# One more attention job of logits ahead of the values: three jobs behind instead of two

## The chip, the cores and the metric

The program runs on one core of a Trainium2 chip. The time is the device time of one execution in microseconds (us), from start to end on that core. Engines are named as in the profile: PE (TensorE) multiplies matrices, DVE (VectorE) and POOL (GpSimd) do elementwise work, ACT (ScalarE) evaluates functions, SP (SyncE) issues transfers. Each engine works through its own instructions in order and waits on semaphores where the program says so.

## The reference

One layer of a hybrid encoder over 2048 prompt tokens and 32 sample tokens that continue a stream of 1024. What matters here is the attention branch: for each query, an indexer scores all visible keys, the best 256 are kept, and eight heads (two key heads with four query heads each) attend to those keys with a relative-position bias.

```python
score = jnp.einsum('bqh,bqhk->bqk', wiblk, jax.nn.relu(dots)) * INDEX_SCALE
_, sel = lax.top_k(score, topk)                       # topk = 256
bias = rel_bias[_t5_bucket(sel - qpos[None, :, None])]
logits = jnp.einsum('bqgrd,bqkgd->bqgrk', qg, ks) * ATTN_SCALE + bias
p = jax.nn.softmax(logits, axis=-1)
o = jnp.einsum('bqgrk,bqkgd->bqgrd', p, vs)
mixed = jnp.concatenate([y_a * silu(gate_a), y_b * silu(gate_b)], axis=-1)
out = jnp.einsum('ble,ed->bld', mixed, w_out)         # then RMSNorm, plus x
```

## The kernel before, in words

Everything up to the indexer's scores is done in a first phase, which the change does not touch. The second phase (`phase2`) starts in the trace at about 957 us and does the attention. Queries come in 17 tiles of 128 (16 of the prompt, t = 0 to 15, and the sample as t = 16), taken in nine groups: p = 0 to 7 hold two tiles each, p = 8 the sample. A tile t of the prompt sees t + 1 tiles of 128 keys; the sample sees nine.

For each group PE first computes row maxima of the logits (`max_logits`, line 1402), mixed with the output projection of the group before (`output`, L1456), and DVE reduces them (`maxima`, L1548). Then comes `attention(p)`, called a stage below. A stage is a list of jobs: for each tile t, for each of the two key heads kv, for each key tile kt, one job. So groups 0 to 8 have 6, 14, 22, 30, 38, 46, 54, 62 and 18 jobs. A job k is:

- `logits` on PE: four matmuls into one PSUM bank (L1416, L1417, L1418, L1421): the high and the low part of the queries, the mask, and the negated maxima. There are two banks, so job k waits until the exponential of job k - 2 has read its bank.
- the exponential on ACT (L1364) from the bank into one of four buffers `E`. ACT waits for the logits, and for the values multiply of job k - 4, which frees the buffer.
- for a near job (its key tile at most five behind the query tile) a multiply of `E` by the bias table on POOL (L1240). 174 of the 290 jobs are near, the last ones of each (t, kv).
- `weighted_values` on PE (L1432; two passes): it adds the values weighted by `E` into one half of `wide[0]`.

When the last job of a (t, kv) is through, ACT copies the sums out of `wide[0]` (`take_sums`: L1261 and L1263). It stands in ACT's order behind the exponential of job last + 2 and waits for the values multiply of job last; where the stage ends before that, it stands at the stage's end. The last `take_sums` of a tile lets DVE invert the denominators (L1562). Three more things share ACT's order. The high part of the queries of tile t + 2 (`high`, L1252) stands behind tile t's last exponential and waits for a transfer that SP issues once the last logits of tile t are done. Pieces of the top-256 search of group p + 2 (counts at L1298, steps at L1310 and L1319) stand in groups 2 to 6 in between the exponentials: 15 to 29 pieces in a stage. And at a group's start come two copies and two squares of the projected output.

DVE's order in group p: part of the search of group p, the denominators of the first tile of group p - 1, the last six search rounds and `set_mask` of the first tile of group p, the denominators of the second tile of p - 1, `set_mask` of the second tile, then the maxima of group p.

Of the kernel before, what the change touches and what calls it, by code (L numbers as in the profile page):

```python
# [46 lines left out]
C_U, C_GA, C_Q, C_K, C_V, C_QI, C_KI, C_WI, C_GB = 0, 512, 1024, 1536, 1664, 1792, 2048, 2080, 2088  # L47
COLS = 2600
BIAS_TILES = 6
BIAS_W = BIAS_TILES * P  # L50
GLEN = BIAS_W + P - 1
MASKED = -1e30
# [18 lines left out]
def key_tiles(t):  # L71
    return t + 1 if t < NPT else PAST // P + 1


def place_of(t):

    return t if t < NPT else PAST // P
# [875 lines left out]
def phase2(nc, A, sb, sem, identf, identb, onesb, kT, unit, banks, wide, q_dram, gb_dram, ma_dram, s_dram, m_dram,  # L953
# [13 lines left out]
    def near(t, kt):  # L967

        return place_of(t) - kt < BIAS_TILES

# [13 lines left out]
    def jobs(p):  # L984
        return [(t, kv, kt) for t in group(p) for kv in range(NKV) for kt in range(key_tiles(t))]
# [23 lines left out]
    with ExitStack() as st:  # L1009
# [3 lines left out]
        vx = sb(st, "vx", [P, NPT, 3, HD], F32)  # L1013
        EB = sb(st, "EB", [P, NH, BIAS_W], F32)
        relb = sb(st, "relb", [NBUCKETS, NH], F32)
# [71 lines left out]
        with nc.Block() as block:  # L1087
            @block.sync
            def _(sp):
# [33 lines left out]
                for kv in range(NKV):  # L1123
# [15 lines left out]

                sp.dma_start(EB[:], bass.AP(g_dram.tensor, P - 1, [[GLEN - 1, P], [P * GLEN, NH], [1, BIAS_W]]))\  # L1140
                  .then_inc(eb_in, 16)
# [235 lines left out]
            def _(pe):  # L1377
# [27 lines left out]
                def logits(t, kv, kt):  # L1405


                    k = fl[t, kv, kt]
                    if kv == 0 and kt == 0:
                        pe.wait_ge(q_split, 2 * t + 2)  # L1410
                        pe.wait_ge(shift_done, t + 1)
                    if k >= 2:
                        pe.wait_ge(fl_free, k - 1)
                    bank = banks[2 + k % 2][:].rearrange("p (j n) -> p j n", j=GRP)
                    keys = k2[kv][:, kt * P:(kt + 1) * P]
                    pe.matmul(bank, keys, qh[:, t % 2, kv], start=True, stop=False)  # L1416
                    pe.matmul(bank, keys, ql[:, t % 2, kv], start=False, stop=False)  # L1417
                    pe.matmul(bank, mask[:, t % 2, kt * P:(kt + 1) * P],  # L1418
                              identb[:].rearrange("p (a n) -> p a n", a=1).broadcast_to([P, GRP, P]),
                              start=False, stop=False)  # L1420
                    pe.matmul(bank, onesb[:], shift[:, t % 2, kv * GRP:(kv + 1) * GRP], start=False, stop=True)\  # L1421
                      .then_inc(fl_full, 1)

                def weighted_values(t, kv, kt):
                    k = fl[t, kv, kt]
                    if near(t, kt):
                        pe.wait_ge(biased, near_count[t, kv, kt])
                    else:
                        pe.wait_ge(fl_free, k + 1)
                    if kt == 0 and t >= 1:  # L1430
                        pe.wait_ge(sums_out, 4 * (t - 1) + 2 * (kv + 1))
                    pe.matmul(wide[0][:, kv * 512:(kv + 1) * 512], vx[:, kt, kv:kv + 2, :].rearrange("p a d -> p (a d)"),  # L1432
                              E[:, k % 4].rearrange("p j n -> p (j n)"), start=(kt == 0),
                              stop=(kt == key_tiles(t) - 1)).then_inc(pv_step, 1)

                def attention(p):
                    todo = jobs(p)
                    if p == 0:
                        pe.wait_ge(v_in, 32)
                    for i in range(len(todo) + 2):  # L1440
                        if i < len(todo):
                            logits(*todo[i])
                        if 2 <= i:
                            weighted_values(*todo[i - 2])

                def output(t, i, c):

# [13 lines left out]
                for p in range(NGR + 1):  # L1461

                    outs = [(t, i, c) for t in group(p - 1) for i in range(2) for c in range(DC)]
                    maxs = [(t, h, c) for t in group(p) for h in range(NH) for c in range(len(chunks(t)))]
                    if p >= NGR - 1:
                        for o in outs:
                            output(*o)
                        outs = []
                    for i, x in enumerate(maxs):
                        max_logits(*x)  # L1470
                        if i % 2 and i // 2 < len(outs):
                            output(*outs[i // 2])
                    for o in outs[len(maxs) // 2:]:
                        output(*o)
                    attention(p)
# [196 lines left out]
```

## Time and profile before

| what | value |
|---|---|
| median of 3 runs | 2189.1 us (2186.41 to 2192.36) |
| the profiled execution | 2185.78 us, its span 2184.0 us |
| PE busy in the span | 1692.6 us |
| DVE busy | 1326.4 us |
| ACT busy | 778.5 us |
| POOL busy | 444.6 us |

The nine stages of the attention, as stretches of the trace (mean clock of PE as a share of full speed):

| stage | from, to (us) | length | jobs | PE busy | ACT busy | clock |
|---|---|---|---|---|---|---|
| 0 | 1056.8, 1093.4 | 36.6 | 6 | 15.67 | 7.97 | 0.69 |
| 1 | 1138.9, 1174.2 | 35.3 | 14 | 30.31 | 13.82 | 0.85 |
| 2 | 1217.8, 1274.5 | 56.7 | 22 | 45.31 | 53.90 | 0.94 |
| 3 | 1336.1, 1400.6 | 64.5 | 30 | 57.54 | 61.64 | 0.97 |
| 4 | 1469.3, 1546.3 | 77.0 | 38 | 71.15 | 71.01 | 0.98 |
| 5 | 1617.4, 1712.6 | 95.2 | 46 | 86.77 | 79.51 | 0.94 |
| 6 | 1780.5, 1888.7 | 108.2 | 54 | 100.45 | 53.76 | 0.97 |
| 7 | 1957.2, 2069.7 | 112.5 | 62 | 111.15 | 42.59 | 1.00 |
| 8 | 2120.3, 2154.9 | 34.6 | 18 | 34.23 | 11.94 | 0.94 |

Busy time counts an instruction from its start to its end, and the ends of matmuls are modelled, so consecutive matmuls overlap in it. A figure behind an arrow is the idle time of an engine just before an instruction, with the instruction that ended it.

### The profile page before, as it was taken

The page shows a single profiled execution, that of the slowest core. Times are in us where ns is not written, and L with a number is a line of the kernel's source. Part 1 is how long each engine was busy: PE and PEld are TensorE (multiplying, and loading weights), DVE is VectorE, ACT ScalarE, POOL GpSimd, SP SyncE. Part 2 cuts the span into 40 slices and gives each one's busy share as a digit, 9 for nine tenths or more (in the row PEclk, how much of TensorE's full clock was granted, in tenths as well). Part 3 has the DMA queues.
Part 4 walks back from the last instruction along what each step waited for, and adds up shares of the span by engine and source line. Part 5 has one row for each costly group of instructions (what it writes and reads, how often), then busy time and mean ns, then how long its engine had stood idle before and what let it go on. Part 6 is the DMA issues. An engine that isn't in the chain of part 4 may idle for free.

```text
span 2184.0 us, 17266 instructions
## 1 busy us (share of the span) xinstructions
PE 1692.6 (78%) x5139; PEld 872.7 (40%) x5175; DVE 1326.4 (61%) x2921; ACT 778.5 (36%) x1419; POOL 444.6 (20%) x336
## 2 busy tenths in 40 slices
PE   3998998879968996820377859679589699599987
PEld 2444554444544552710133324234244244244433
DVE  4222655767774556130794298888997988883431
ACT  2112222323333443120113837639369245213312
POOL 0001000000010000010225342604404504503404
PEclk9999899999989997955688989889799799799989
DMA  6001100201010101044612120020110100100010
GB/s 271 22 22 44 42 33 35 63 29 46 30 36 37 38 35 50 17 121 55 212 49 74 29 75 20 10 98 12 60 46 10 59 20 10 48 20 0 20 60 24
DMA packets 80672, 108.43 MB, mean 50 GB/s; under 512 B 15286, under 2 KB 58646, under 8 KB 80195
## 3 DMA queue, kind: packets, MB, share of 16 engines
q1 hardware_dynamic: 80578, 107.32, 15.7%
q8 instruction: 42, 0.69, 0.1%
q14 instruction: 52, 0.42, 0.1%
HBM read 67.16 MB, written 39.09 MB: 49 GB/s over the span
## 4 chain that ended last, share of the span: by engine, by line
PE 26%; DVE 15%; issue 7%; another core or an unknown queue 3%; ACT 3%; POOL 2%; DMA 1%; SPq 1%; POOLq 0%; DVEq 0%; ACTq 0%
PE wide L1456 7%; PE wide L1432 7%; PE bank L1402 3%; DVE reach L293 2%; DVE above L293 2%; PE bank L1416 2%; PE bank L1417 2%; PE bank L1418 2%; DVE S L327 2%; PE bank L1421 2%; DVE den L1562 2%; ACT act_junk L1298 1%; POOL E L1240 1%; DVE reach L331 1%
## 5 line engine op out<-in xcount | busy, mean ns | idle before, releaser
L683 PE MATMUL bank<-hT,W 128*128 128x512 f32 (+1 forms) x1280 | 497.9, 539 | 2.1 <-DVE gst L871 2.1
L1240 POOL TENSOR_TENSOR E<-E,EB 128x512 f32<-128x512 f32 x174 | 241.6, 1398 | 679.8 <-ACT E L1364 678.6
L1402 PE MATMUL bank<-k,qh 128*128 128x512 f32 (+3 forms) x344 | 170.0, 551 | 230.0 <-DVE mxp L1548 209.9
L1432 PE MATMUL wide<-E,vx 128*128 128x512 f32 x580 | 309.4, 618 | 20.3 <-POOL E L1240 18.6
L683 PEld LDWEIGHTS bank<-hT,W 128*128 128x128 f32 x1280 | 225.0, 193 | 221.7 <-issue 213.5
L1548 DVE CUSTOM_DVE_ANT_0 above<-bank,mask 128x512 bf16<-128x512 f32 (+3 forms) x344 | 195.4, 605 | 161.3 <-DMA bias_scratch<-reach 81.3
L1416 PE MATMUL bank<-qh,k 128*128 128x512 f32 x290 | 228.3, 787 | 49.8 <-ACT E L1364 47.5
L663 ACT ACTIVATE relu<-wide 128x1024 f32<-128x1024 f32 (+7 forms) x208 | 155.2, 765 | 232.8 <-PE wide L698 196.0
L1364 ACT ACTIVATE E<-bank 128x512 f32<-128x512 f32 x290 | 170.8, 593 | 187.6 <-PE bank L1421 138.4
L919 DVE SCALAR_TENSOR_TENSOR S<-relu,wi,S 128x1024 f32<-128x1024 f32 (+7 forms) x182 | 169.4, 960 | 98.4 <-ACT relu L663 97.9
L1402 PEld LDWEIGHTS bank<-k,qh 128*128 128x128 f32 x344 | 71.4, 210 | 354.0 <-DVE mxp L1548 321.2
L698 PE MATMUL wide<-kiT,qiT 96*128 96x512 f32 (+3 forms) x344 | 162.7, 548 | 17.1 <-ACT relu L663 16.9
L1562 DVE RECIPROCAL den<-den 128x512 f32<-128x512 f32 x17 | 56.8, 3346 | 192.7 <-ACT den L1263 192.7
L1298 ACT ACTIVATE act_junk<-S,minus_cand 128x1152 bf16<-128x1152 f32 (+3 forms) x108 | 170.9, 1582 | 0.8
L1349 ACT ACTIVATE sq<-wide 128x512 bf16<-128x512 f32 x34 | 20.3, 597 | 373.7 <-PE wide L1456 373.7
L683 PE MATMUL bank<-W,hT 128*128 128x296 f32 (+1 forms) x544 | 151.1, 416 | 1.5 <-DVE W L795 0.8
L293 DVE TENSOR_SCALAR_CACHE_REDUCE above<-S,search 128x1152 bf16<-128x1152 f32 (+4 forms) x91 | 141.8, 1558 | 3.0
L1432 PEld LDWEIGHTS wide<-E,vx 128*128 128x128 f32 x580 | 109.8, 195 | 81.8 <-POOL E L1240 44.6
L1456 PE MATMUL wide<-wout,ma 128*128 128x512 f32 x272 | 142.0, 632 | 0.0
L1456 PE MATMUL wide<-wout,yT 128*128 128x512 f32 x272 | 135.3, 607 | 6.7 <-POOL yT L1233 6.7
L561 POOL TENSOR_TENSOR win<-U 128x512 f32<-128x512 f32 (+7 forms) x20 | 18.9, 943 | 573.1 <-ACT U L625 573.1
L293 DVE TENSOR_SCALAR_CACHE_REDUCE reach<-S,search 128x1024 bf16<-128x1024 f32 (+4 forms) x78 | 134.1, 1720 | 0.0
(167 smaller groups left out, 2151.2 us busy)
## 6 DMA issues: line engine op xcount, KB each, us to landing
q<-q_scratch SPq DMA_DIRECT2D x68, 128.0 KB, 3.1
xs<-x_prompt SPq DMA_DIRECT2D x16, 512.0 KB, 4.1
xr<-x_prompt SPq DMA_DIRECT2D x16, 512.0 KB, 7.5
y_prompt<-kT SPq DMA_DIRECT2D x16, 512.0 KB, 6.4
W<-w_in SPq DMA_DIRECT2D x8, 768.0 KB, 17.2
gb<-gb_scratch SPq DMA_DIRECT2D x17, 256.0 KB, 7.6
ma<-ma_scratch SPq DMA_DIRECT2D x17, 256.0 KB, 3.2
W<-w_in SPq DMA_DIRECT2D x8, 532.0 KB, 8.5
```

The lines of the kernel that those rows point to most:

```text
L293: dve.tensor_scalar((B.above, B.reach)[i][:, 0:s.shape[1]], s, B.cand[:, i:i + 1], None, ALU.is_ge, ALU.add, accum_out=B.cnt[:, i:i + 1]). ...
L683: mm = pe.matmul(out, stationary(c), moving(c), start=(c == 0), stop=(c == DC - 1))
L698: mm = pe.matmul(wide[k % 2][:, x - a:y - a], qiT[:, t % 2, h, :], kiT[:, x:y], start=True, stop=True)
L919: dve.scalar_tensor_tensor(S[:, t % 2, a:b], relu[:, k % 2, 0:b - a], w, S[:, t % 2, a:b], ALU.mult, ALU.add).then_inc(relu_used, 1)
L1240: pool.tensor_tensor(E[:, k % 4], E[:, k % 4], EB[:, kv * GRP:(kv + 1) * GRP, off:off + P], ALU.mult)\
L1298: act.activation(act_junk[:, 0:w], S[:, slot(p, i), 0:w], ACT.Sign, bias=minus_cand[:, p % 2, i:i + 1], accum_out=act_sum[:, i:i + 1])\
L1364: act.activation(E[:, k % 4], banks[2 + k % 2][:].rearrange("p (j n) -> p j n", j=GRP), ACT.Exp).then_inc(fl_free, 1)
L1402: pe.matmul(banks[k % 2][:, 0:b - a], qh[:, t % 2, kv, j, :], k2[kv][:, a:b], start=True, stop=True)\
L1416: pe.matmul(bank, keys, qh[:, t % 2, kv], start=True, stop=False)
L1432: pe.matmul(wide[0][:, kv * 512:(kv + 1) * 512], vx[:, kt, kv:kv + 2, :].rearrange("p a d -> p (a d)"), E[:, k % 4].rearrange("p j n -> p ...
L1456: mm = pe.matmul(wide[1][:, i * 512:(i + 1) * 512], stat, wout[:, c, i * 512:(i + 1) * 512], start=(c == 0), stop=(c == DC - 1))
L1548: dve.tensor_tensor_reduce(junk[:, k % 2 * 512:k % 2 * 512 + b - a], banks[k % 2][:, 0:b - a], mask[:, t % 2, a:b], 1.0, LEAST, ALU.add, A ...
```

## The change

PE now issues the values multiply of job i - 3 behind the logits of job i, where it was job i - 2. Banks, buffers, semaphores and the orders of all other engines stay.

```diff
+BEHIND = 3
@@ in phase2, the tensor engine's program
                 def attention(p):
                     todo = jobs(p)
                     if p == 0:
                         pe.wait_ge(v_in, 32)
-                    for i in range(len(todo) + 2):
+                    for i in range(len(todo) + BEHIND):
                         if i < len(todo):
                             logits(*todo[i])
-                        if 2 <= i:
-                            weighted_values(*todo[i - 2])
+                        if BEHIND <= i:
+                            weighted_values(*todo[i - BEHIND])
```

## Rows read from the trace of the kernel before

**Rows 1.** The page: engine totals, the chain that ended last, the costliest groups.

```profile
PE 1692.6 (78%) x5139; PEld 872.7 (40%) x5175; DVE 1326.4 (61%) x2921; ACT 778.5 (36%) x1419; POOL 444.6 (20%) x336
PE 26%; DVE 15%; issue 7%; another core or an unknown queue 3%; ACT 3%; POOL 2%; DMA 1%; SPq 1%; POOLq 0%; DVEq 0%; ACTq 0%
...
L1432 PE MATMUL wide<-E,vx 128*128 128x512 f32 x580 | 309.4, 618 | 20.3 <-POOL E L1240 18.6
L1416 PE MATMUL bank<-qh,k 128*128 128x512 f32 x290 | 228.3, 787 | 49.8 <-ACT E L1364 47.5
```

**Rows 2.** Waits of the whole span: who <- for whom: us, times, longest.

```profile
PE bank L1402 <- DVE mxp L1548: 209.9, 36, 67.2
DVE den L1562 <- ACT den L1263: 192.7, 11, 32.3
```

**Rows 3.** Timeline of stage 7, two jobs, PE and ACT: start, duration, instruction.

```profile
1984.00 0.80 PE L1416 MATMUL bank<-qh,k 128*128 128x512 f32 x1
1985.52 0.60 ACT L1364 ACTIVATE E<-bank 128x512 f32<-128x512 f32 x1 [1.18 <-PE bank L1421]
1985.78 0.80 PE L1416 MATMUL bank<-qh,k 128*128 128x512 f32 x1
...
1986.38 0.59 ACT L1261 ACTIVATE osum<-wide 64x512 f32<-64x512 f32 x1 [0.26 <-PE wide L1432]
1987.61 0.60 ACT L1364 ACTIVATE E<-bank 128x512 f32<-128x512 f32 x1
```

**Rows 4.** Timeline of stage 7: POOL's bias multiply and PE's values multiply of steady jobs.

```profile
1977.33 1.28 POOL L1240 TENSOR_TENSOR E<-E,EB 128x512 f32<-128x512 f32 x1 [0.49 <-ACT E L1364]
1980.00 1.02 PE L1432 MATMUL wide<-E,vx 128*128 128x512 f32 x2
```

**Rows 5.** Timeline of stage 4 around its first taking of sums.

```profile
1491.43 0.80 PE L1416 MATMUL bank<-qh,k 128*128 128x512 f32 x1
1493.81 0.59 ACT L1261 ACTIVATE osum<-wide 64x512 f32<-64x512 f32 x1 [0.21 <-PE wide L1432]
1494.92 1.67 ACT L1298 ACTIVATE act_junk<-S,minus_cand 128x1664 bf16<-128x1664 f32 x1
1497.36 0.50 PE L1416 MATMUL bank<-qh,k 128*128 128x512 f32 x1
```

**Rows 6.** Timeline: DVE's denominators of first tiles (stages 4, 6) and stage 6's second.

```profile
1512.31 3.35 DVE L1562 RECIPROCAL den<-den 128x512 f32<-128x512 f32 x1 [9.60 <-ACT den L1263]
1835.38 3.35 DVE L1562 RECIPROCAL den<-den 128x512 f32<-128x512 f32 x1 [7.49 <-ACT den L1263]
1890.03 3.35 DVE L1562 RECIPROCAL den<-den 128x512 f32<-128x512 f32 x1 [4.53 <-ACT den L1263]
```

**Rows 7.** Timeline of stage 4: third and fourth logits, and the middle taking of sums.

```profile
1476.10 0.79 PE L1416 MATMUL bank<-qh,k 128*128 128x512 f32 x1 [4.38 <-ACT E L1364]
1478.92 0.90 PE L1416 MATMUL bank<-qh,k 128*128 128x512 f32 x1
...
1508.02 0.80 PE L1416 MATMUL bank<-qh,k 128*128 128x512 f32 x1
1511.07 0.59 ACT L1261 ACTIVATE osum<-wide 64x512 f32<-64x512 f32 x1
```

**Rows 8.** Timeline of stage 1: logits of its eleventh job, and `high`.

```profile
1163.41 1.41 PE L1416 MATMUL bank<-qh,k 128*128 128x512 f32 x1
1176.05 1.06 ACT L1252 ACTIVATE qh<-q 128x1024 fp32r<-128x1024 f32 x1 [4.41 <-DMA q<-q_scratch]
```

**Rows 9.** A stretch of stage 1: length, PE busy, clock, DMA share, GB/s.

```profile
1155.00:1166.00 11.00, 8.98 (x18) 0.54 0.00 0
```

**Rows 10.** Timeline: POOL at the end of stage 6; PE behind stage 7's end.

```profile
1872.97 13.65 POOL L1240 TENSOR_TENSOR E<-E,EB 128x512 f32<-128x512 f32 x5 [0.49 <-ACT E L1364]
2068.55 1.13 PE L1432 MATMUL wide<-E,vx 128*128 128x512 f32 x2 [0.31 <-POOL E L1240]
2075.82 4.54 PE L1456 MATMUL wide<-wout,yT 128*128 128x512 f32 x6 [2.71 <-POOL yT L1233]
```

## The prediction

> **What bounds the kernel now.** I read the page first. PE is the busiest engine (1692.6 of 2184.0 us), yet the chain that ended last holds only 26% of PE and 15% of DVE [rows 1]: the two hand the work to each other. PE stood still 20.3 us before the values multiply, mostly for POOL's bias multiply, and 49.8 us before the logits, mostly for ACT's exponential [rows 1]. These are the two waits that the change can touch. The waits of the whole span then say who hands over to whom: PE waits 209.9 us for DVE's maxima, and DVE waits 192.7 us for the sums that ACT takes out of PSUM [rows 2].
>
> So I went stage by stage, through the timeline, asking what the next stage waits for. In stages 2 to 5 DVE sits idle until the sums of the group's *first* tile come, in the middle of the stage (9.60 us in stage 4 [rows 6]); behind them stand the last search rounds, two masks and the maxima, and PE, done with its stage, waits for those. There the second half of the stage is off the path, and the first half, up to the taking of sums, is on it. In stage 6 DVE waits for the first tile (7.49 us) and again for the second (4.53 us [rows 6]), so the end of the stage counts. In stages 7 and 8 the end counts too. In stage 1 the end counts by another way: last logits, SP's transfer of the queries, ACT's `high` at 1176.05, and only then the last sums [rows 8]. Stage 0 is hidden: DVE is in a long run of search rounds and takes up the sums late.
>
> **A steady job.** In stage 7 nothing disturbs. Logits start at 1984.00 and 1985.78: 1.78 us a job, about 0.9 for the logits and 0.9 for the values. The exponential starts 1.52 us behind its logits (1985.52) and lasts 0.60 [rows 3], the bias multiply 1.28 [rows 4]. The one that began at 1977.33 ended at 1978.61, and the values multiply of the same job began at 1980.00: 1.4 us to spare, with the change one cadence more, 3.2 us. That removes waits only where POOL or ACT is late by 1.4 us or more.
>
> **What the change moves.** Values of job k go one logits later. Counted from PE's start of a stage, logits come 0.9 us earlier (one values multiply fewer ahead) and each values multiply 0.9 later. PE's own work is the same, so nothing is won or lost on PE unless a wait changes. Buffer `E` has four parts, and the exponential of job k waits for values k - 4, which PE still issues just ahead of logits k: no new wait there.
>
> *The taking of sums is what changes.* It waits for values `last` and stands in ACT's order behind exponential last + 2. Before, PE issues those values right behind logits last + 2, and the sums are taken 2.38 us after these logits start (1986.38 less 1984.00 [rows 3]), a wait of 0.26. After, values last - 1, logits last + 3 and values last come behind: one cadence more, 4.16 us. ACT stands idle 1.78 us longer, and behind it are queued exponential last + 3 and, in stages 2 to 6, search pieces. Exponential last + 3 ended 4.21 after the reference logits (1988.21); now 4.21 + 1.78 = 5.99. Logits last + 5 need its bank and are due at 3 x 1.78 = 5.33: PE stalls 0.7. Where a search piece is queued in between, as in stage 4 (1.67 us), logits last + 5 start 5.93 after the reference (1497.36 less 1491.43 [rows 5]), a stall of 0.6 already; the full 1.78 is then added. Each pair of tiles has three such places inside its stage, the sample one. The fourth stands at the end and waits only for PE's last values.
>
> *The start of a stage.* In stages 2 to 6 the third logits wait 3 to 5 us for ACT, which is still at squares and search pieces (4.38 us in stage 4 [rows 7]). The fourth start at 1478.92, behind values 0. After the change they can't follow before the second exponential is read, at about 1478.35, so of the 0.9 only about 0.5 is won; the bounds are 0 and 0.9. I take 0.5.
>
> Sum, stage by stage, as the shift of what the path waits for:
>
> - Stage 0: 0. Bounds -0.5 and +0.5.
> - Stage 1: logits there run at 3.4 us a job (start of the eleventh job at 1163.41 [rows 8], of the tenth at 1159.98) since the clock is 0.54, partly at the lower level of 1.2 GHz [rows 9], behind 3.2 us of idling. PE waits 1.1 us for the bias multiply there, which is then covered, and each values multiply that moves back is worth 1.7 at that clock. The logits of the eleventh job should start at 1161.9: -1.5, which SP, the transfer and `high` pass on. Bounds -2.5 and 0.
> - Stage 2: ACT is nearly full (53.9 of 56.7 us). The first sums were taken 2.9 after the reference logits, so they slip by 1.3 less 0.7; the sums of the first tile's second head follow at +1.2. Bounds 0 and +2.5.
> - Stage 3: also full of search pieces (61.64 of 64.5 us); the first delay of 1.78 runs through ACT's queue: +1.9. Bounds +0.5 and +3.
> - Stages 4 and 5, each: -0.5 for the start, +1.78 at the first sums, and at the middle ones, which were taken 3.05 us behind logits already (1511.07 less 1508.02 [rows 7]), 4.16 - 3.05 = +1.1. Together +2.4. Bounds +0.7 and +3.5. The second tile's sums, late too, just about stay hidden.
> - Stage 6: the end counts. Two stalls of 0.7 and one with a search piece of 1.8: +3.2. POOL works without a break through the last five bias multiplies, 13.65 us instead of 5 x 1.28 [rows 10], since DVE's mask work for two inputs runs beside it; these start with the logits, 0.5 earlier. PE's waits of 4.2 us for POOL there look like a gain for the change, but the last values need the last bias multiply wherever they stand. +2.7. Bounds 0 and +4.
> - Stage 7: three stalls of 0.7 = +2.1; won back are 1.25 us at two jobs whose bias multiply was slow, and 0.9 of earlier logits, since PE's wait behind the stage goes over POOL's last multiplies (2.71 us at 2075.82 [rows 10]). +0.1. Bounds -1 and +2.
> - Stage 8: one stall of 0.7, less the 0.3 that PE waits for POOL before the last values of a stage (0.31 in stage 7 [rows 10]), which is covered now. +0.4. Bounds -0.3 and +0.8.
>
> Sum: -1.5 + 1.2 + 1.9 + 2.4 + 2.4 + 2.7 + 0.1 + 0.4 = +9.6 us. The profiled execution took 2185.8 (span 2184.0 and 1.8 around it), so its like would take 2195.4. It lies 3.3 below the median of the runs, so I add the sum to the median: 2189.1 + 9.6 = 2198.7 us.
>
> **A rule against this.** PE is the busiest engine and its idle time before the values is 20.3 us [rows 1]. The Trainium skill, Perfetto Trace Analysis, section Identifying the Most-Contended Engine with Optimization Strategy, says to optimize the engine of highest occupancy, find its gaps and make what they wait for come sooner. By this rule the change, which gives POOL one job more, would win up to those 20 us. It is the first rival.
>
> **The rivals.**
>
> - *PE's waits for POOL go and nothing takes their place: faster.* For it: 20.3 us of idling before the values, none over 3.35 us at a time, so mostly coverable. Against it: what of it lies in halves of stages that the path leaves out (4.4 us in stage 2, 3.4 at the end of stage 5), or behind POOL's own unbroken row (4.2 in stage 6). If it all counted and ACT's queue took the later sums without stalls, 2189.1 - 18 = 2171; with half of it on the path, 2180. It decides if the sums cost under 0.3 us each.
> - *ACT's delay is absorbed: no change.* ACT idles in stages 6 to 8 (53.76 of 108.2 us busy in stage 6), DVE's chain from the first tile's sums is the path of four stages, and if the first sums' delay dies out before the second ones, each of these stages has only the 0.9 of one logits less 0.5: 4 x 0.4, with stage 6 at +1 and stage 1 at -1.5 it is +1 to +3: 2191.
> - *The clock pays too: slower still.* After the idling at a stage's start the clock is down for some us (stage 1, 0.54 [rows 9]). PE idles about 1 us more between third and fourth logits. If the lower clock lasts one job longer in five stages, 5 x 0.9 = 4.5 more: 2203.
>
> **How the numbers follow.** The forecast has a chance of 0.50, the third rival 0.12, no change by absorption 0.30, the faster one 0.08. A measurement of this kernel can tell about 0.3%, 6.6 us, from no change: slower means above 2195.7, faster below 2182.5. Slower by over 0.3% has 0.12 and, of the forecast whose own range is 2194 to 2203, nearly all: 0.60. Within 0.3%: 0.32. Faster: 0.08. The range 2189 to 2206 takes in most of the absorbed case and of the clock case and leaves out the faster one.
>
> **What would show it.** In the changed kernel's timeline of stage 7 the first sums (L1261) should be taken 4.16 us after the logits of two jobs past the last, with 2.0 us of ACT idling ahead of them instead of 0.26, and PE's third logits behind should show a wait of 0.7 for ACT. PE's idling before the values should fall from 20.3 to under 10 us, and that before the logits rise from 49.8 by 25 or more. DVE's wait in stage 4 for the first tile should grow by about 2.4. Wrong if ACT's idling before the sums stays under 1 us, if PE shows no new wait for ACT in stage 7, or if DVE's denominators come no later relative to their stage's start.

## The result and the profile after

The change made the kernel slightly slower: 2193.0 us (median of 20 runs, 2186.97 to 2198.35) against 2187.3 (20 runs), a ratio of 1.0023 with a 95% interval of 1.0016 to 1.0031, so 3.5 to 6.8 us. The profiled execution of the changed kernel took 2198.4 us, the highest of its 20 times. All line numbers of the changed file are one higher than before (L1433 is the values multiply, L1417 the first logits matmul, L1262 the taking of sums).

The page of the changed kernel: engine totals, the values multiply and the first logits matmul with the idle time before them. They answer to [rows 1].

```profile
PE 1704.8 (78%) x5175; PEld 878.0 (40%) x5175; DVE 1328.1 (60%) x2921; ACT 777.3 (35%) x1419; POOL 445.1 (20%) x336
...
L1433 PE MATMUL wide<-E,vx 128*128 128x512 f32 x580 | 305.1, 613 | 13.5 <-POOL E L1241 13.3
L1417 PE MATMUL bank<-qh,k 128*128 128x512 f32 x290 | 221.5, 764 | 69.5 <-ACT E L1365 65.7
```

The wait that the change shortens did get shorter, 20.3 to 13.5 us, and the wait for ACT grew from 49.8 to 69.5. Why shows in the waits of the changed kernel from 1056 us on (who <- for whom: us, times, longest):

```profile
DVE den L1563 <- ACT den L1264: 198.7, 11, 32.5
...
ACT osum L1262 <- PE wide L1433: 71.2, 31, 7.9
```

The row of the kernel before, over the same part of the span:

```profile
ACT osum L1261 <- PE wide L1432: 25.6, 21, 6.6
```

ACT stood still 71.2 us before the sums; it was 25.6 us before the change. DVE's own wait for them grew from the 192.7 of [rows 2].

The timeline of the changed kernel at the first taking of sums in stage 4, which answers to [rows 5]:

```profile
1500.13 0.80 PE L1417 MATMUL bank<-qh,k 128*128 128x512 f32 x1
...
1502.51 0.59 ACT L1262 ACTIVATE osum<-wide 64x512 f32<-64x512 f32 x1 [1.99 <-PE wide L1433]
1503.62 1.67 ACT L1299 ACTIVATE act_junk<-S,minus_cand 128x1664 bf16<-128x1664 f32 x1
1505.40 1.09 ACT L1365 ACTIVATE E<-bank 128x512 f32<-128x512 f32 x2
1506.06 0.50 PE L1417 MATMUL bank<-qh,k 128*128 128x512 f32 x1 [1.81 <-ACT E L1365]
```

Read from ACT's side: 1.99 us of idling, then the sums, a search count that stands in between, and only then the exponential that frees a bank. PE idled 1.81 us for it. The row at 1500.13 is already the logits of job last + 3; those of last + 2 began at 1498.36, so the sums came 4.15 us behind them.

I timed each stage from its first logits to those of the next one (stage 8 to the end of the span); these are differences of starts in the timelines:

| stage | before | changed | changed, again | forecast shift | shift (again) |
|---|---|---|---|---|---|
| start of stage 0 | 1056.8 | 1060.1 | 1056.8 | 0 | 0.0 |
| 0 | 82.1 | 85.1 | 83.5 | 0 | +1.4 |
| 1 | 78.9 | 74.8 | 74.5 | -1.5 | -4.5 |
| 2 | 118.3 | 120.9 | 120.8 | +1.2 | +2.5 |
| 3 | 133.2 | 134.2 | 134.1 | +1.9 | +0.9 |
| 4 | 148.0 | 151.0 | 150.9 | +2.4 | +2.9 |
| 5 | 163.1 | 166.8 | 166.8 | +2.4 | +3.6 |
| 6 | 176.7 | 179.2 | 179.2 | +2.7 | +2.6 |
| 7 | 163.1 | 160.3 | 160.3 | +0.1 | -2.8 |
| 8 | 63.7 | 64.1 | 64.2 | +0.4 | +0.5 |
| span | 2184.0 | 2196.6 | 2191.1 | +9.6 | +7.1 |

"Again" is the first experiment below. The two profiles of the changed kernel agree to 0.1 us in stages 2 to 8; they differ in the first phase, which the change doesn't touch (3.3 us), and in stages 0 and 1. So single profiles of this kernel can be compared stage by stage though their spans can't. One limit: the on-time version below differs by 2.5 us in stage 3 between its own two profiles.

### The profile page after: what moved, and what is told of

It reads as the page before. It is cut to its first block, busy times and chain, and to the rows that moved or that the text cites. A ratio compares the mean times of both kernels' runs of the same rounds, so it can differ in the third digit from the quotient of the medians.

```text
span 2196.6 us, 17302 instructions
## 1 busy us (share of the span) xinstructions
PE 1704.8 (78%) x5175; PEld 878.0 (40%) x5175; DVE 1328.1 (60%) x2921; ACT 777.3 (35%) x1419; POOL 445.1 (20%) x336
## 4 chain that ended last, share of the span: by engine, by line
PE 27%; DVE 14%; issue 7%; another core or an unknown queue 3%; ACT 3%; DMA 1%; POOL 1%; SPq 1%; POOLq 0%; DVEq 0%; ACTq 0%
PE wide L1457 8%; PE wide L1433 7%; PE bank L1403 3%; DVE reach L294 2%; PE bank L1417 2%; DVE above L294 2%; PE bank L1418 2%; PE bank L1419 2%; PE bank L1422 2%; DVE S L328 2%; DVE den L1563 2%; ACT act_junk L1299 1%; DVE reach L332 1%; DVE above L322 1%
## 5 line engine op out<-in xcount | busy, mean ns | idle before, releaser
L1241 POOL TENSOR_TENSOR E<-E,EB 128x512 f32<-128x512 f32 x174 | 246.8, 1429 | 694.1 <-ACT E L1365 693.5
L1433 PE MATMUL wide<-E,vx 128*128 128x512 f32 x580 | 305.1, 613 | 13.5 <-POOL E L1241 13.3
L1417 PE MATMUL bank<-qh,k 128*128 128x512 f32 x290 | 221.5, 764 | 69.5 <-ACT E L1365 65.7
L1350 ACT ACTIVATE sq<-wide 128x512 bf16<-128x512 f32 x34 | 20.3, 597 | 366.8 <-PE wide L1457 366.8
L1433 PEld LDWEIGHTS wide<-E,vx 128*128 128x128 f32 x580 | 112.6, 196 | 71.9 <-POOL E L1241 27.8
L294 DVE TENSOR_SCALAR_CACHE_REDUCE reach<-S,search 128x1024 bf16<-128x1024 f32 (+4 forms) x78 | 134.1, 1719 | 0.0
```

The lines of the kernel that those rows point to most:

```text
L294: dve.tensor_scalar((B.above, B.reach)[i][:, 0:s.shape[1]], s, B.cand[:, i:i + 1], None, ALU.is_ge, ALU.add, accum_out=B.cnt[:, i:i + 1]). ...
L1241: pool.tensor_tensor(E[:, k % 4], E[:, k % 4], EB[:, kv * GRP:(kv + 1) * GRP, off:off + P], ALU.mult)\
```

## The experiments

**The changed kernel again.** No edit.

> The changed kernel once more, for a second profile and a second size. The profile of the changed kernel had 2198.4 us, the highest of its 20 times (median 2193.0, before 2187.3), so its stages can't be read for sizes alone. Theory A (the sums are taken one job later, ACT idles, PE and DVE wait for it in stages 2 to 6; stages 1 and 7 win something back): again 4 to 7 us over the kernel before; in the profile ACT idles about 2.0 us before the sums in stage 7, the first tile's denominators come 1 to 3.7 us later from the start of stages 2 to 5, and stage 1 is shorter by 3 us or more. Theory B (the difference lies in the stage starts, the clock, and chance meetings of DVE with POOL): these shifts differ by more than 2 us from the first profile, in sign too.

Measured: 2192.6 us (2190.93 to 2197.8), ratio 1.0027 (1.0017 to 1.0036). The stages are in the table: every sign and, from stage 2 on, every length came again. For stages 1 and 7 the later runs add to this. Stage 7 took 160.3, 160.3 and 160.5 us in the profiles with plain three behind there, and 163.1 in both with the kernel's old order there. With three behind and the bias multiply in place, stage 1 took 73.9 to 74.8 us in eight profiles and 76.6 to 76.7 in two, against 78.9 before. Stage 0 tells nothing: with its old order it took 82.1 us in one profile and 83.7 in another.

**Three behind, but the sums on time.** The decisive one: it keeps the distance of three and takes away only the lateness of each last values multiply.

```diff
-                    for i in range(len(todo) + BEHIND):
+                    done = 0
+                    for i in range(len(todo) + BEHIND):
                         if i < len(todo):
                             logits(*todo[i])
-                        if BEHIND <= i:
-                            weighted_values(*todo[i - BEHIND])
+                        upto = min(max(i - BEHIND + 1, 0), len(todo))
+                        if 2 <= i < len(todo) and todo[i - 2][2] == key_tiles(todo[i - 2][0]) - 1:
+                            upto = max(upto, i - 1)
+                        while done < upto:
+                            weighted_values(*todo[done])
+                            done += 1
```

> Three behind, but the values of the last job of each tile and key head are issued where two behind would have issued them (behind the logits of job last + 2), so that the sums are taken as early as before; all other jobs keep the distance of three. Theory A: the price goes and what was won stays: ACT idles 0.3 us before the sums again, stages 2 to 6 are back to their old lengths or 0.5 us shorter, stage 1 stays 3 us or more shorter: 2179 to 2185, 3 to 8 us under the kernel before. Theory B: no difference from three behind, 2191 to 2195.

Measured: 2179.2 us, ratio 0.9964 (0.9953 to 0.9974), 8.4 us under the kernel before and 13.4 under the changed one on the same chip. In stage 7 the first sums are taken 29.20 us after its start (29.22 before, 30.12 in the changed kernel).

```profile
1985.92 0.59 ACT L1262 ACTIVATE osum<-wide 64x512 f32<-64x512 f32 x1 [1.12 <-PE wide L1433]
```

ACT idles 1.12 us before them, not the 0.3 that I had put down: its exponential is through earlier, by the one values multiply that no longer stands ahead of the logits. Against the kernel before, stage 1 was 4.7 us shorter, stage 7 3.5 and stage 6 0.2. Stages 2, 4 and 5 stayed 0.5 to 0.6 us longer and stage 3 3.1, where I had expected the old lengths or less ("Where the start of a stage loses", below). Its page:

```profile
L1433 PE MATMUL wide<-E,vx 128*128 128x512 f32 x580 | 298.6, 607 | 13.3 <-POOL E L1241 11.7
L1417 PE MATMUL bank<-qh,k 128*128 128x512 f32 x290 | 218.8, 754 | 57.6 <-ACT E L1365 55.3
```

The wait for POOL is as short as in the changed kernel (13.5); more than half of the added wait for ACT is gone (49.8, 69.5, now 57.6). So the distance of three, with the sums on time, is a gain, and the late sums turn it into a loss.

**Two behind, the sums one job late.** The other half: PE's order of before, and only ACT's wait moved.

```diff
-                def take_sums(t, kv):
+                def take_sums(t, kv, more=0):
-                    act.wait_ge(pv_step, last_fl(t, kv) + 1)
+                    act.wait_ge(pv_step, last_fl(t, kv) + 1 + more)
...
                         while waiting and last_fl(*waiting[0]) <= k - 2:
-                            take_sums(*waiting.pop(0))
+                            take_sums(*waiting.pop(0), 1)
```

> Two behind as before, and only ACT's wait is changed: inside a stage it takes the sums when the values of job last + 1 are through instead of job last. PE's order is untouched, ACT idles 1.77 us longer at 25 places. Theory A: this alone costs more than the change did, since nothing is won by the order: stages 2 to 6 some 1.8 to 3.2 us each, stage 7 some 1.3: 12 to 16 us in all, 2199 to 2203. Theory B: at most 3 us, under 2190.

Measured: 2202.8 us, ratio 1.0074 (1.0059 to 1.0089), 15.3 us over the kernel before. Its waits:

```profile
DVE den L1562 <- ACT den L1263: 214.6, 12, 34.5
...
ACT osum L1261 <- PE wide L1432: 77.6, 31, 6.5
PE bank L1416 <- ACT E L1364: 61.9, 23, 18.2
```

A like idling of ACT (77.6 us) without the gains of the new order costs 15 us. By the stages, 2, 4, 5 and 6 are 4.0, 3.6, 3.6 and 2.8 us longer than before and stage 7 1.1. Stage 3 is not (-0.2), though its first tile's denominators come 2.1 us later; the reason is that of the changed kernel's stage 3, below. Together with the run before, the price is shown from both sides.

**Three behind in the outer stages only** (0, 1, 7, 8).

```diff
+                    behind = 2 if 2 <= p <= 6 else BEHIND
-                    for i in range(len(todo) + BEHIND):
+                    for i in range(len(todo) + behind):
...
-                        if BEHIND <= i:
-                            weighted_values(*todo[i - BEHIND])
+                        if behind <= i:
+                            weighted_values(*todo[i - behind])
```

> Three behind in stages 0, 1, 7 and 8, two behind in stages 2 to 6. Theory A: the winning stages keep their win (stage 1 about 4, stage 7 about 0.6 at its end) and the losing ones are as before: 2180 to 2184, some 3 to 6 us under the kernel before. Theory B: between -2 and +2 of the kernel before.

Measured: 2181.5 us, ratio 0.9975 (0.9965 to 0.9984), 6.0 under the kernel before. The shifts of the table for stages 0, 1, 7 and 8 add up to 5.4 under, near that. Its own profile fits less well: stage 1 took 76.7 us there, 2.3 less than before and not 4.5, with 6.8 us at the lower clock instead of 3.4.

**The sums one exponential later in ACT's order.**

```diff
-                        while waiting and last_fl(*waiting[0]) <= k - 2:
+                        while waiting and last_fl(*waiting[0]) <= k - 3:
```

> Three behind as in the change, but in ACT's order the sums stand one exponential later (behind that of job last + 3), so that ACT no longer idles for the last values with the next exponential queued behind it. The sums themselves are taken no earlier. Theory A has two parts: the lateness of the sums, which stays, and the idling of ACT, which goes. So stage 7 loses its three small stalls (0.4 us each), stages 4 and 5 lose theirs (up to 1.8 each), and the first tile's denominators in stages 2 to 5 still come some 1 us later than with two behind: 2182 to 2188, between the on-time version (2179.2) and the change (2192.6). If only the lateness of the sums cost, and not the blocked exponential: 2191 to 2194.

Measured: 2188.5 us, ratio 1.0008 (0.9999 to 1.0017): 4 us better than the change, 0.5 above the range that I had given, and no better than before. ACT's wait before the sums is 24.3 us, as it was before, and stage 7 ends earlier (last sums at 110.73 us instead of 111.95). So both parts of the theory hold, the blocked exponential and the lateness. One stage went another way: stage 5 took 168.5 us, 1.7 more than with the change, though its sums came earlier. From the first denominators to the second DVE took 52.9 us there and 46.7 before. Its rows over that stretch (L328 is the scan, L298 and L301 the small search steps; busy us and mean ns):

```profile
L328 DVE TENSOR_TENSOR_SCAN S<-reach,above 128x1664 f32<-128x1664 bf16 x1 | 5.6, 5591 | 0.0
...
L298 DVE TENSOR_SCALAR search<-search 128x2 f32<-128x2 f32 x6 | 3.8, 639 | 0.2
L301 DVE SCALAR_TENSOR_TENSOR search<-search,search 128x2 f32<-128x2 f32 x6 | 3.1, 520 | 0.2
```

Operations on two numbers a partition last 0.16 to 0.17 us when nothing is in their way; here they average 0.5 to 0.6. What is in their way is told below.

**No bias multiply on POOL**, with two and with three behind, one profiled execution each. The softmax then lacks the bias. The edit is the same in both: neither POOL's multiply nor PE's wait for it is issued, and PE waits for the exponential alone.

```diff
-                        if near(t, kt):
+                        if False:
                             k = fl[t, kv, kt]
...
-                    if near(t, kt):
+                    if False:
                         pe.wait_ge(biased, near_count[t, kv, kt])
```

> Two behind; POOL's bias multiply is left out altogether, so the bias is missing from the softmax. The pair to the next kernel. Without it PE never waits for POOL in a stage, and if DVE's small operations of 1.1 us are held up by POOL's bias multiply (39 of 39 in the kernel before overlap one and end with it), none of them is left over 0.4 us while the stages run.

> Three behind, POOL's bias multiply left out as in the kernel with two behind. Theory A: what the change costs has nothing to do with POOL, so the difference to two behind without bias is at least what it is with it: 5 to 11 us longer span, with the same 2.0 us of idling before the sums. If the cost came from POOL meeting DVE elsewhere in time, the two spans differ by less than 3 us.

Measured: spans of 2148.7 and 2167.3 us, a difference of 18.6, over the 5 to 11 that I had expected, with the 2.0 us of idling before the sums as expected; 2.8 of it lie in the first phase, 3.5 in stage 0, and stages 1 to 8 make 12.4 (-0.6, -0.1, +3.5, +3.5, +2.8, +0.8, +1.2, +1.5). With the bias multiply the same stages made +5.7. So without the bias multiply the change is a plain loss in these two profiles, and most of what it wins in the real kernel is won against POOL: the gains of stages 1 and 7 (-4.5 and -2.8) are -0.6 and +1.2 without it. The small DVE operations over 0.9 us fell from 28 in the stages to none with two behind and two with three (those meet POOL's `low`, L1202 in that file). Stage 3 shows the loss undisturbed: its denominators come 3.3 us later, DVE takes 36.8 us from the first to the second in both, and the stage is 3.5 longer.

**Where the start of a stage loses.** Two versions with the sums on time: two behind in stages 2 to 5, and two behind for the first eight jobs of stages 2 to 6.

```diff
-                    done = 0
-                    for i in range(len(todo) + BEHIND):
+                    done, behind = 0, 2 if 2 <= p <= 5 else BEHIND
+                    for i in range(len(todo) + behind):
...
# the other version, in the loop
+                        behind = 2 if 2 <= p <= 6 and i < 8 else BEHIND
...
```

> Sums on time, two behind in stages 2 to 5, three behind in the others. In the profile of the on-time version stage 3 was 3.1 us longer than before and stages 2, 4 and 5 0.5 each, with the longer stretch of PE's lower clock at the start of stages 3 and 4 (6.8 us instead of 3.4). Theory A with the clock as third part: these four go back to their old lengths and the rest keeps its win: 2173 to 2177. If stage 3's length was chance: 2178 to 2181.

> Sums on time; in stages 2 to 6 the first eight jobs are two behind, all later ones three. Tells whether the loss in stages 3 and 4 comes from PE's idling between third and fourth logits at the start (clock theory: the first sums of stage 3 are again taken 20.7 us after its start and not 22.8, those of stage 4 24.5 and not 26.8; 2172 to 2178), or from the distance of three in the middle of the stage, where ACT is full (then they stay at 22.8 and 26.8, and the time near 2179).

Measured: 2179.3 us (ratio 0.9961, 0.9949 to 0.9974) and 2179.8 us (0.9964, 0.9951 to 0.9976). The times missed what the clock theory forecast in both cases and equal the plain on-time version, as its rivals said; the profiles met the theory: the first sums of stage 3 are taken 20.70 us after its start in both (22.79 in the on-time version, 20.71 before), those of stage 4 24.5 in both (26.8; 24.5). To settle this I ran the first of them and the on-time version side by side.

> The version with two behind in stages 2 to 5, sums on time, once more, beside the plain on-time version on the same chip. Their times were equal (2179.3 and 2179.2), though by the stages the first should be 3 us shorter (stage 3 by 3.0, stages 4 and 5 by 0.4 and 0.5). If the stages tell the truth: 2 to 4 us under the next kernel. If not: within 1 us of it.

> The plain on-time version once more, 2178 to 2180.5; see the kernel with two behind in the middle stages for what is told apart.

Measured: 2177.4 us (5 runs, ratio 0.9963, 0.9950 to 0.9975) and 2182.3 us (11 runs, 0.9982, 0.9973 to 0.9991). Two in the middle is 4.9 us ahead here and was 0.2 behind before. One thing that varies is in the on-time version itself, whose stage 3 took 136.3 us in its first profile and 133.8 in its second. A stretch of 12 us at the start of stage 3 in its first profile (length, PE busy, granted clock, DMA share, GB/s):

```profile
1336.00:1348.00 12.00, 9.44 (x23) 0.72 0.07 19
```

and in its second profile, the same stretch:

```profile
1336.00:1348.00 12.00, 9.09 (x27) 0.86 0.11 28
```

The stage began at 1331.7 and 1332.1. PE has just idled 3.9 us in both, and its clock is at the lower level for 6.8 us of the first stretch and 3.4 of the second, in the same program. The first sums are taken 22.8 and 21.1 us after the stage's start, so 1.7 of the 2.1 us that they were late is this spell. All eight profiles with two behind at the start of stage 3 have the shorter spell; of the six with three behind, two have it. But this does not explain the medians: the profile with the shorter stage 3 belongs to the set of runs in which the on-time version was slower (2182.3), and in it stages 2 to 5 take 563.9 us together, against 563.6 in both profiles of two in the middle. What two in the middle is worth stays open, between 0 and 5 us, and so does the cause of the 4.9.

**Three behind in stage 1 alone.** The edit is that of the outer stages with `behind = BEHIND if p == 1 else 2`.

> Three behind in stage 1 alone, two behind in all others. In the traces stage 1 (to the start of stage 2) is 4.1 to 4.5 us shorter with three behind, and PE's lower clock lasts 3.4 us in it instead of 10.2. If that is the whole story, the time is 3.5 to 4.5 us under the kernel before, 2183 to 2184.5. If a shorter stage 1 is given back in stage 2 (DVE or ACT late there), it is within 1.5 us of the kernel before.

Measured: 2183.6 us, ratio 0.9988 (0.9979 to 0.9997), 2.9 us under the kernel before, below the 3.5 expected, with the interval reaching 4.6. Stage 1 took 74.5 us, all stages from 2 on were as before to 0.15 us. Nothing is given back.

## Why the prediction was half right

The sign, the mechanism and the range held: I forecast 2198.7 us with 2189 to 2206, and 2193.0 came. The size did not: +9.6 us against +5 to +5.7 in the medians, and I had given 0.60 to a slowing of over 0.3%, where it came out within. (Of the 5.7 us between forecast and result, 1.8 come from the base, a median of 3 runs.) The terms that failed are those of stages 1 and 7.

- *The taking of sums* was right in its place and nearly in its numbers: 4.16 us forecast, 4.15 measured; idling 2.0 forecast, 1.99 to 2.04 measured where ACT was not still at a search piece. The stall in a stage without search pieces was 0.42 us and not 0.7. The late logits did start 6.03 us after the reference, near the 5.99 forecast; but their second matmul follows 0.34 us behind the first and not the 0.64 of the steady row, so of the 0.7 only 0.42 is left. Over six such places this is 1.7 us less.
- *The signs.* PE's idling before the values fell to 13.5 us and not under 10, that before the logits rose by 19.7 and not 25, and DVE's wait in stage 4 grew from 9.60 to 14.55 us, by 5.0 and not 2.4: the mechanism is there, these sizes were off too.
- *Stage 1, the failed step.* I priced the covered wait for POOL at the clock that the trace of before showed, -1.5 us, with -2.5 as the bound. But the clock was a result of these waits. A stretch of stage 1 in the changed kernel, which answers to [rows 9] (its stage began 6.4 us later; both stretches hold the start of the spell of lower clock):

```profile
1155.00:1166.00 11.00, 8.09 (x20) 0.84 0.17 49
```

  PE idled 2.8 us there, where before it idled 3.2 for ACT and soon after 1.1 for POOL, and its clock stayed at the lower level for 3.4 us instead of 10.2. Stage 1 won 4.1 us, and 4.5 in the second profile. In two other profiles with three behind the spell was 6.8 us, and the win only 2.3. Without the bias multiply the spell is 3.4 us and the stage 75.3 us long with two behind already.
- *Stage 7, the same error.* I had +0.1; it was -2.8. The end of the stage came 0.6 earlier; the rest is the output projection behind it. [rows 10] shows six of its first eight matmuls; here are all eight, before and in the changed kernel:

```profile
2075.82 5.40 PE L1456 MATMUL wide<-wout,yT 128*128 128x512 f32 x8 [2.71 <-POOL yT L1233]
...
2089.89 3.70 PE L1457 MATMUL wide<-wout,yT 128*128 128x512 f32 x8 [2.43 <-POOL yT L1234]
```

  That is 1.7 us less for the same eight. The spell of 3.4 us at the lower clock that stood there before is gone. Together stages 1 and 7 are 5.9 us of the sum: had they come as priced, the "again" profile would have shown +13.
- *Stages 2 to 6* were to be +10.6 and were +12.5. Stage 4's denominators of the first tile came 3.7 us later, not 2.4 (43.0 and 46.7 us after its start). The 1.3 us more come from the start: the fourth logits of stage 4 do come 0.57 us earlier, as forecast, but those behind which the first sums are taken come 1.1 us later in stage 4 and 1.6 in stage 3, where I had 0.5 earlier. The lower clock lasts 6.8 us there instead of 3.4, which I had only as the third rival, with 0.12. It is true of stages 3 and 4 and not of 2, 5 and 6.
- *Stage 3* came out shorter (+0.9) in spite of denominators 3.4 us later: DVE met POOL less often behind them (three small operations over 0.9 us in the stage instead of six; see the last section). From the first to the second denominators it took 37.1 us instead of 40.7, and 3.3 of the 3.6 lie in the search's small steps (L297, L300). In stage 4 it took 44.5 instead of 46.7. So it is in part luck that the sum of stages 2 to 6 came near: later starts that I had not priced stand against shorter stretches of DVE that I had not priced either.
- *The first rival* is refuted as it stood: PE's waits for POOL shrank by 6.8 us and the time grew. By the rule of the Trainium skill, Perfetto Trace Analysis, section Identifying the Most-Contended Engine with Optimization Strategy, that gap was the one to close, and the on-time version (8.4 us under the kernel before) agrees, with one condition: what is moved must hold nothing that another engine's queue waits for.
- *Absorption* is refuted as a mechanism: ACT has idle time in stage 7 and still PE stalls. The class that it stood for, within 0.3%, is the one that came, for another reason.

## What to carry to other kernels

When a pipeline is made one step deeper, look at what waits for the last item of a group, not at the steady state: here 25 hand-overs moved one job back and turned a gain of 8 us into a loss of 5. Keep the distance for the bulk and issue the last item of each group early. And where a trace shows a stretch at the lower clock, don't price a change with it: ask whether the idling that caused the lower clock goes.

## What the runs showed of the hardware

A DVE operation on two numbers a partition that begins while POOL's bias multiply is running does not finish before that multiply does. In the kernel before, 39 such operations lasted 0.36 to 1.27 us instead of 0.16 to 0.17, and all 39 begin during a bias multiply and end within 0.03 us of its end. (One that began in the same instant as a multiply took 0.16.) Here are two of them:

```profile
1260.77 2.51 POOL L1240 TENSOR_TENSOR E<-E,EB 128x512 f32<-128x512 f32 x2 [0.54 <-ACT E L1364]
...
1261.23 0.85 DVE L297 TENSOR_SCALAR search<-search 128x2 f32<-128x2 f32 x1
...
1262.11 1.19 DVE L300 SCALAR_TENSOR_TENSOR search<-search,search 128x2 f32<-128x2 f32 x1
```

The two multiplies end at 1262.05 and 1263.28, the two small operations at 1262.08 and 1263.30. The large counts beside them (L293, 128x1024 with an accumulator) last 1.27 us whether POOL works or not. One-input operations on a single number a partition are not held either: four that begin during a bias multiply take the 0.15 us that they take elsewhere. Since the search's small steps stand one behind the other, each such meeting is up to 1.1 us on DVE's path, and a change of order on PE moves which ones meet. The Trainium skill, GPSIMD Engine Reference, section Key points, says that POOL shares its SBUF interfaces with DVE, with contention when a DVE instruction has two inputs in SBUF or runs in a two-port mode. The trace agrees for the two-input one (L300, 1.19 us instead of 0.16). It shows that the one-input operation on two numbers is held as well (L297, 0.85 us); in which mode that one runs, no row tells. Leaving the bias multiply out took 35.3 us off the span with two behind (one profile each), more than all of PE's waits for it (20.3 us before the values).
